# A hybrid decoder layer: attention's preparation stage reordered and loaded ahead, its compressed branch spread over more steps

## The reference, cut to what matters

```
z = rmsnorm(x) @ w_in                      # q, and k, v for three branches, and gates
kcmp = gelu(blocks(kc) + pos) @ w1) @ w2   # 127 overlapping blocks of 32 keys, stride 16
p_c  = softmax(q . kcmp - slope * dist)    # compressed branch; also ranks the key blocks
imp  = sum over heads of p_c @ overlap     # importance of each 64-key block
sel  = top 8 blocks by imp (first and the last two forced)
o_sel = softmax(q . ks[sel]) @ vs[sel]     # selected branch
o_win = softmax(q . kw[last 512]) @ vw     # sliding window branch
o = g0 * (p_c @ vcmp) + g1 * o_sel + g2 * o_win
```

## Time and profile before

| | us |
|---|---|
| median of 3 runs | 4378.86 |
| the runs | 4370.42 to 4383.64 |
| the profiled execution | 4383.34 |
| its span | 4381.6 |

### The profile page before, as it was taken

One profiled execution on the slowest core, in us unless ns is written; L12 is line 12 of the kernel. 1 busy time (PEld: TensorE's weight loads), 2 busy tenths in 40 slices (PEclk: granted clock), 3 DMA queues, 4 the chain that ended last, 5 costly groups with the idle time before them and its releaser, 6 DMA issues. The chain is left out here.

```text
span 4381.6 us, 69853 instructions
## 1 busy us (share of the span) xinstructions
PE 3901.1 (89%) x26848; PEld 3193.6 (73%) x26849; DVE 2436.0 (56%) x4140; ACT 1983.5 (45%) x3138; POOL 553.1 (13%) x842
## 2 busy tenths in 40 slices
PE   7899999999989857888888986999599999999698
PEld 5687877777767636777776775899478888888487
DVE  2454555555555425777776754444567555567465
ACT  2433333343333314666665653222166555567465
POOL 0111112111121102111111111000110000000110
PEclk9999999999999967999999977999699999999799
DMA  4443443443333250000000005333288666679542
GB/s 131 132 117 100 128 108 100 128 109 86 106 91 80 66 116 25 15 15 10 20 18 20 21 12 160 132 116 123 89 336 326 233 233 232 234 295 394 191 148 91
DMA packets 512951, 557.22 MB, mean 127 GB/s; under 512 B 106284, under 2 KB 374572, under 8 KB 511628
## 3 DMA queue, kind: packets, MB, share of 16 engines
q1 hardware_dynamic: 471476, 457.94, 32.7%
q0 software_dynamic: 16416, 59.78, 3.6%
q10 hardware_dynamic: 24784, 35.71, 2.5%
HBM read 439.78 MB, written 113.57 MB: 126 GB/s over the span
## 5 line engine op out<-in xcount | busy, mean ns | idle before, releaser
L523 PE MATMUL fr_fb<-fr_hT_h,fr_w_h 128*128 128x512 f32 (+1 forms) x1312 | 531.9, 405 | 7.7 <-DVE fr_hT_r L978 6.0
L523 PE MATMUL fr_fb<-fr_hT_h,fr_w_r 128*128 128x512 f32 (+1 forms) x1312 | 530.8, 405 | 0.0
L523 PE MATMUL fr_fb<-fr_hT_r,fr_w_h 128*128 128x512 f32 (+1 forms) x1312 | 530.8, 405 | 0.0
L958 DVE TENSOR_TENSOR fr_w_r<-fr_w_raw,fr_w_h 128x1024 fp32r<-128x1024 f32 (+1 forms) x164 | 198.0, 1208 | 491.3 <-ACT fr_w_h L774 490.2
L1950 DVE TENSOR_TENSOR aq_p_lo<-aq_t_bank,aq_p_hi 128x512 fp32r<-128x512 f32 x412 | 282.7, 689 | 200.2 <-ACT aq_p_hi L1842 193.5
L1842 ACT CAST aq_p_hi<-aq_t_bank 128x512 fp32r<-128x512 f32 x412 | 237.6, 580 | 256.0 <-PE aq_t_bank L1747 252.7
L798 ACT COPY fr_zs<-fr_fb 128x512 f32<-128x512 f32 (+1 forms) x148 | 87.0, 588 | 506.6 <-PE fr_fb L523 506.2
L523 PEld LDWEIGHTS fr_fb<-fr_hT_h,fr_w_h 128*128 128x128 f32 (+1 forms) x1312 | 248.0, 189 | 71.8 <-issue 10.4
L523 PEld LDWEIGHTS fr_fb<-fr_hT_h,fr_w_r 128*128 128x128 f32 (+1 forms) x1312 | 248.2, 189 | 63.2 <-issue 11.0
L523 PEld LDWEIGHTS fr_fb<-fr_hT_r,fr_w_h 128*128 128x128 f32 (+1 forms) x1312 | 248.3, 189 | 61.6 <-issue 9.6
L134 PE MATMUL ex_gu<-wx_gate_w,ex_xT 128*128 128x512 f32 x1176 | 288.5, 401 | 3.7 <-DVE ex_xT L2706 3.6
(11 more groups left out here) (474 smaller groups left out, 8758.8 us busy)
## 6 DMA issues: line engine op xcount, KB each, us to landing
wx_raw<-in_w_exp_gate_up SPq DMA_DIRECT2D x64, 2048.0 KB, 10.6
fr_w_raw<-in_w_in SPq DMA_DIRECT2D x160, 512.0 KB, 3.9
wx_raw<-in_w_exp_down SPq DMA_DIRECT2D x32, 2048.0 KB, 11.4
s_z<-fr_zs SPq DMA_DIRECT2D x160, 256.0 KB
s_rows<-ex_y ACTq DMA_DIRECT2D x50, 512.0 KB, 4.3
mx_mg<-s_z SPq DMA_DIRECT2D x32, 512.0 KB, 7.2
fr_zc<-s_z SPq DMA_DIRECT2D x15, 903.0 KB, 6.7
fr_x_t<-in_x SPq DMA_DIRECT2D x16, 512.0 KB, 5.3
```

What stands on the lines that cost most here:

```text
L523: ins = pe.matmul(bank[0:cols_, :], (w_h, w_h, w_r)[p][:, k, c, 0:cols_].bitcast(F32R), (hT_h, hT_r, hT_h)[p][:, c, :].bitcast(F32R), star ...
L958: dve.tensor_tensor(w_r[:, m % 2, :, 0:cols_].bitcast(F32R), w_raw[:, m % 2, :, 0:cols_], w_h[:, m % 2, :, 0:cols_], ALU.subtract).then_in ...
```

## The change

Three things are changed.

**The early loads.** x_t becomes a buffer `shared` that outlives the first stage. At the start of chunk 13 SP loads w1 and pos into its free part (eight DMAs, of 1024 pieces each: 256 B for w1, 4 B for pos). Later the tables t_sel, t_cmp, keep_t and force_t and the queries qf lie in the same buffer.

**The stage in front of attention in another order.** SP loads kv for k first, then v_raw, the first queries, k 0 and 1, gates, second queries, k 2 and 3; ACT loads kv for v. Each load has a semaphore of its own. TensorE starts with the 32 products of pos, then the 32 of kv, then values and the second layer. ACT applies the gelu first, then casts all eight groups of values, then the keys. GpSimd builds the tables and splits two query tiles here, and only t_sel is left for attention. `tab_ok` is gone.

**The plan.** TABLE_STEPS goes from 7 to 8, and scores, exps, inverse, normalise and turn stand 10, 9, 7, 6 and 4 steps before out.

```diff
@@ first stage, SP
             for c in range(NCH):
+                if c == NCH - 3:
+                    sync.wait_ge(filled, last_turn[NQ - 1] + 1)
+                    for a, n in enumerate(("k", "v")):
+                        for d in range(2):
+                            own = slice(d * HD, (d + 1) * HD)
+                            sync.dma_start(early["w1"][own, a, :, :], A[f"cmp_{n}_w1"][0].rearrange("(l d) e -> d l e", d=HD)[:, d * L_HALF:(d + 1) * L_HALF, :]).then_inc(early["in_w1"], 16)
+                            sync.dma_start(early["pos"][own, a, :], A[f"cmp_pos_{n}"][0].rearrange("l d -> d l")[:, d * L_HALF:(d + 1) * L_HALF]).then_inc(early["in_w1"], 16)
@@ stage in front of attention, SP
+                load_kv(sync, 0)
                 for br in range(2):
-                    sync.dma_start(v_raw[:, br, :], Z["z"][KINDS[br][1]:KINDS[br][1] + P, :]).then_inc(in_v, 16)
+                    sync.dma_start(v_raw[:, br, :], Z["z"][KINDS[br][1]:KINDS[br][1] + P, :]).then_inc(in_v[br], 16)
+                load_raw(sync, 0)
+                load_qf(sync, 0)
                 load_k(0)
                 load_k(1)
...
+                load_raw(sync, 1)
                 load_k(2)
                 load_k(3)
+                for o in range(1, QF):
+                    load_qf(sync, o)
@@ stage in front of attention, ACT after the change
+                load_kv(act, 1)
+                act.dma_start(w2_v[:, :], A["cmp_v_w2"][0]).then_inc(in_w, 16)
...
+                act.wait_ge(pos_made, 2)
+                for a in range(2):
+                    act.copy(pos_p[:, a:a + 1], out[0:HD, POS + a:POS + a + 1]).then_inc(pos_ok, 1)
+                for a in range(2):
+                    act.wait_ge(hid_made, a + 1)
...
+                for n in range(8):
+                    act.wait_ge(turned, n + 1)
...
+                high(0)
+                high(1)
+                act.wait_ge(g_ok, 1)
+                act.activation(gates[:, :, :], gates[:, :, :], ACT.Sigmoid).then_inc(g_done, 1)
+                high(2)
+                high(3)
@@ GpSimd: behind the tables, now in the stage in front
-                pool.sem_inc(tab_ok, 1)
+                split_q(pool, 0)
+                split_q(pool, 1)
@@ Plan
-    Y_RING, FRONTS_APART, TABLE_STEPS = 3, 7, 7
+    Y_RING, FRONTS_APART, TABLE_STEPS = 3, 7, 8
...
-            marks += [(out - 8, 0, n, "scores", t, g), (out - 2, 1, n, "turn", t, g), (out, 2, n, "out", t, g)]
-            marks += [(out - 7, 0.3, n, "exps", t, g), (out - 5, 0.6, n, "inverse", t, g)]
-            pool += [(out - 4, 0, n, "normalise", t, g), (self.begin[self.at[t, g, SEL]] - 2, 1, n, "bias", t, g)]
+            marks += [(out - 10, 0, n, "scores", t, g), (out - 4, 1, n, "turn", t, g), (out, 2, n, "out", t, g)]
+            marks += [(out - 9, 0.3, n, "exps", t, g), (out - 7, 0.6, n, "inverse", t, g)]
+            pool += [(out - 6, 0, n, "normalise", t, g), (self.begin[self.at[t, g, SEL]] - 2, 1, n, "bias", t, g)]
```

429 lines of the change are left out of this document (214 added, 215 removed).

## The result

The changed kernel takes 4328.8 us (median of 4 runs, 4320.1 to 4331.4); the kernel before takes 4374.6 in the same comparison (4 runs, 4367.7 to 4383.6). The ratio is 0.9881, 95% interval 0.9862 to 0.9901: faster by 1.2%. Forecast were 4340 and a range of 4317 to 4366.

The account below looks back on a forecast made before the run. TensorE is busy for 89% of the span, so time is to be had where it idles or runs at half clock. -23.7 + 2.2 - 18 + 1 = -38.5 us from a median of 4378.9 gives 4340; range 4317 to 4366.

Parts of the forecast that it names:

- The mechanism of the stage: Stage in front of attention: kv products start at 1590.5, key reloads become the tail, attention's first matmul 23.7 us sooner.
- Attention's start: First pair in attention: inverse ahead of the masks makes DVE wait for ACT's table load and exps, +2.2 us.
- The plan: Attention: fewer TensorE waits at turn and turn_y, -13 us, and more time at full clock, -5; together -18 us.
- The two thirds: Attention: of nominally 19 us of saved TensorE waits, two thirds were taken to come through, -13 us.
- Rival B: Attention: the waits only move and the new plan gives nothing, 4358 us; chance 0.18.
- the clock: Attention: a third of some 30 low-clock places at the turns keeps its clock, -5 us, bounds 0 and -15.
- The first stage: First stage: eight early loads of 8192 packets hold SP, tight at inverses_out; +1 us, bounds 0 and +8.
- rival F: First stage: small packets drain slowly on SP's queue and inverses_out waits; 4410 us at 100 packets per us; chance 0.05.
- part 1: Step-by-step forecast of the stage in front of attention, from its loads to attention's first matmul: -23.7 us.
- the stage's term: Change in time to attention's first matmul: -23.7 us, or -32 without kv split over SP and ACT.
- rival C: Stage in front of attention: the rates of the two queues add up, 8.5 us more gained, 4332 us; chance 0.10.
- Rival E: The stage in front of attention doesn't get shorter, transfers setting its length; half of the wait gain, 4366 or more; chance 0.09.

Follow-up runs that it names:

- e6: Kernel before with only the early loads of w1 and pos in the first stage added: 4371.7 us, ratio 0.9997.
- e1: Changed kernel with attention's old plan (distances 8, 7, 5, 4, 2, table steps 7): 4341.2 us, ratio 0.9933 to the kernel before.
- e2: Kernel before with attention's new plan alone (distances 10, 9, 7, 6, 4, table steps 8): 4358.7 us, ratio 0.9962.
- e8: Changed kernel with attention's old plan, but turn 3 steps ahead of out instead of 2: 4383.0 us, ratio 1.0016 to the kernel before.
- e3: Changed kernel with w1 and pos loaded in the stage itself on ACT's queue, not early: 4358.0 us, ratio 0.9967 to the kernel before.
- e4: Changed kernel with kv for v on SP's queue behind kv for k, instead of on ACT's: 4320.7 us, ratio 0.9888 to the kernel before.

## Why the prediction was right

**The mechanism of the stage** was right, and the shape of it: kv first, no wait on GpSimd, the reload of keys 2 and 3 as the new tail, DVE's split of key 3 as the last work. Two terms were off, by 5.7 us together. The products were forecast to start at 1590.5, when kv for k and v had both landed; they need only k's half, which landed at 17.9 us after the start instead of 21.5 (-3.7), and v's had landed when its turn came. From the last product to attention's first matmul 29.2 were forecast and 26.9 came (-2.3): gelu and casts of values took 5.4 us to the first cast of a key, where 7.4 were taken. What the prediction had as the reason for the wait in the kernel before, ACT's own issues of 12.69 and 8.93 us, was a half only: e6 takes them away and the stage stays at 98.7, because TensorE has the products of kv behind gates that land late.

**Attention's start**: +2.2 were forecast for the inverse in front of the masks; first transposes came 10.4 us behind the first matmul instead of 9.5 (9.2 in e1, the new stage with the old plan). DVE did wait 1.71 us for ACT's exps, its reciprocal at 1645.28 and the first mask at 1645.38 behind it; about 1 us of that reached TensorE. In e2, where the tables are still made in attention, it is 11.9, the forecast's size.

**The plan**: -18 forecast, -17.7 on the mean of all profiles; -13 as waits and -5 as clock forecast, -13.1 and -4.4 measured. In the sum of waits, turn fell from 28.5 to 1.0, and turn_y went from 14.0 (on ACT) to 13.5 (on DVE), as counted. Missing in the count was `out`: 8.0 us more behind a back (0.2 before, 8.2 after), though no such neighbour one step apart was new, and 2.5 behind a turn_y, a neighbour left out. Too high was scores behind a back, 5.7 counted and 2.0 measured. All waits on the bank together fell from 68.2 to 51.4 us in the two profiles, 17 of the nominal 19.

The two thirds taken of it were right in size and not in reason. The prediction had the rest go to the split of the turned block, but that wait fell too, from 20.3 to 17.1 us. What grew is the product with the values, which waits for ACT's copy of the result before: 18.1 to 18.9 us with the old plan, 25.0 to 26.5 in all eight profiles with the new. The agreement of the -13 is in part luck. Rival B, that the plan gives nothing, is out by e1 and e2.

For the clock, the mechanism (places that keep the higher level) isn't shown for the new plan: 10-us windows with a granted clock below 0.9 are 29, 26 and 22 of 94 with the old plan and 25 to 28 of 92 in six profiles with the new. Only e8 shows the direction, the other way round: 34 of 97, and 16 us more of busy time.

**The first stage**: +1 forecast. From the store that stands just ahead of the eight loads (s_yr) to the stage's end it is 219.3 us after and 217.9 before; but 219.3 in e2 and 219.0 in e3, which have no early loads, and 216.9 to 220.9 in the eleven profiles that have them. A price of 1 us can be neither shown nor excluded in that spread, and there is no larger one. They held SP from 1349.51 to 1359.5; inverses_out went out at 1361.45, 12.6 us behind s_yr where it was 13.5 in the earlier trace rows. So rival F, a slow drain of small packets, didn't happen; e3 shows what it is like with large ones in the other queue.

**The other 15 us** of the profiled difference: 5.7 from the stage, 2.4 from parts that the change doesn't touch, 1.8 from the first stage, and 5.7 in attention, where 3.8 are spread (983.2 lies 2.7 above the mean of its plan, 961.6 lies 1.2 below). The medians differ by 45.8, against 38.5 forecast; the stage's 5.7 and the 1 us of the first stage are most of what is left.

**One queue or two** (the rule weighed in part 1). The prediction had the products start 12 us in with one queue, e4 has them at 13.3; it had -32 for the stage's term, e4 has -32.6. That is no hit of the step itself: against the changed kernel one queue is worth 3.2 us and not 8.5, and the rest is the 5.7 us by which the changed kernel's stage was already better than forecast. That two queues add up (rival C) is out.

**Slips in the sums.** None moves the forecast out of its range. 1.7 us and 18.9 us after 1569.0 are 1589.6, where 1590.5 is taken. 4.06 MB at 367 GB/s would be 7.8 us sooner than at 0.215 MB/us, not 8.5. Rival E's -13 leaves out the +2.2 and the +1: with them it is -9.5, 4369.
